# A two-block transformer kernel: the second layer's adaLN columns summed on VectorE instead of multiplied on TensorE

## The chip, the cores and the metric

The kernel is one program on one core of a Trainium2 chip. The metric is the device time of one execution in microseconds (us), lower is better; the runs shown are three executions of the kernel before. TensorE (PE) multiplies, VectorE (DVE), ScalarE (ACT) and GpSimd (POOL) do the elementwise work, and SyncE's queue (SP) issues the weight transfers.

## What is computed

The reference runs a first block of two layers on 256 latent tokens and 256 context tokens, and then a second block (gated mixing, a linear recurrence and a convolved feed-forward) on the latent tokens. All is fp32, with a model width of 2048. The part that the change touches is the modulation ahead of each layer of the first block:

```
shift, scale, gate = jnp.split(jax.nn.silu(c) @ ada_w[l] + ada_b[l], 3, axis=-1)
shift_c, scale_c, gate_c = jnp.split(jax.nn.silu(c_ctx) @ ada_w[l] + ada_b[l], 3, axis=-1)
h = rmsnorm(x, norm_g[l]) * (1.0 + scale[:, None]) + shift[:, None]
hc = rmsnorm(xc, norm_g[l]) * (1.0 + scale_c) + shift_c
...
x_new = x + gate[:, None] * out
```

Two vectors (`c` and `c_ctx`, 2048 long) are multiplied with a 2048 x 6144 matrix for each of two layers. In the last layer the context's gate is not used.

## The kernel before, in words

All weights stream from memory in chunks of 512 KB into the eight slots of `RAW`. A chunk of a projection ("tm" or "fm") is split by ACT (L1540, the high part) and DVE (L1784, the low part) into one of four `SPL` slots, and PE multiplies it in three products. A chunk of adaLN weights ("ada") isn't split: PE multiplies it from `RAW` with four column tiles side by side (L1289), 256 rows of the matrix and 512 columns at a time. Eight such chunks make a group of 512 columns; there are 12 groups for each layer: 0 to 3 shift, 4 to 7 scale, 8 to 11 gate. When a group is through, ACT copies its sums out of bank 6 (L1550), PE turns them (L1368, four transposes into bank 7), and DVE reduces them and adds the bias (L1814, L1818; L1822 for a scale).

The order of all work is written out by hand, by one planner. `chunks` holds the chunks in the order in which PE takes them; `run_chunks` walks it, and at each chunk it lets `run_ahead` put the loads and splits of coming chunks (up to five positions ahead, ada chunks counted), pops side tasks from `hi` and `low` (norms, rope, attention in rows of four stages, pooling, Fourier maps) and puts the matmuls. Each engine works off the one list `order` in that order, so whatever stands ahead on an engine's list comes first. A `RAW` slot is loaded again when the chunk eight places earlier has been split or multiplied (`load_ahead`); the loads stand in one queue, in chunk order.

The stretches of `chunks` are these. The first holds the first layer's eight shift and scale groups and the first k and v projection (72 chunks). Then come 64 projection chunks of the first layer (queries, pooling, Fourier, and from the 33rd on the gates), mixed by `mixed` with 64 ada chunks: two projection chunks, two ada chunks, and so on. Then 28 chunks of the output projection, mixed with 28 ada chunks, and four of it alone, which are multiplied in two passes (latent rows last). Then `FILL` = 4 ada chunks alone. Then the second layer's 72 projection chunks (two groups of queries, 16 chunks; k and v, 8; pooling, 8; Fourier, 8; gates, 32), mixed two and two with the last 32 ada chunks. A projection chunk of the first layer is 24 matmuls of 512 columns, one of the second layer's query, pooling and Fourier groups is 12.

At the second layer's start, each of the tiles of h is made by DVE (L1828), ACT (L1558, L1561) and POOL (L2237), and PE waits for them in order. `STAT`, `TMP` and the like are small buffers; `CW` holds silu(c) and silu(c_ctx) as columns.

Of the kernel before, what the change touches and what calls it, by code (L numbers as in the profile page):

```python
# [17 lines left out]
NRAW = 8  # L18
NSPL = 4
AHEAD = 5  # L20
START_AHEAD = 3
FILL = 4
# [37 lines left out]
def two_block_program(nc, I, out):  # L60
    es = ExitStack()
    with es:
# [114 lines left out]
        s_tab, s_dft = [sem(f"rope{l}_in") for l in range(2)], [sem(f"dft{l}_in") for l in range(2)]  # L177
        s_ap = [sem(f"pool_matrix{l}_in") for l in range(2)]
# [7 lines left out]
        s_adaE, s_adaT, s_adaS, s_ada, s_s2 = sem("ada_out"), sem("ada_turned"), sem("ada_summed"), sem("ada_column"), sem("ada_scale")  # L186
        s_h0, s_h1, s_h1b, s_h2 = sem("h_scaled"), sem("h_hi"), sem("h_shifted"), sem("h_lo")
# [44 lines left out]
        at = {"loaded": 0, "taken": 0, "split": 0, "used": 0, "pos": 0, "ahead": AHEAD}  # L232
# [13 lines left out]
        def multiplied():  # L246
            return (s_chunk, at["pos"])
# [7 lines left out]
        def group(form, stage, W, c0, banks, then, tokens=(), side=1):  # L255
            g = Group(form, stage, banks, tokens, side)
            aps = fm_aps(W, c0) if form == "fm" else tm_aps(W, c0)
            cs = [Chunk(g, kc, ap, {"ada": 0, "tm": 2, "fm": 4}[form]) for kc, ap in enumerate(aps)]
# [3 lines left out]

        def load_ahead():
            while at["loaded"] < len(queue):
                i = at["loaded"] - NRAW
                last = []
                if i >= 0 and queue[i].shape:
                    if i >= at["taken"]:
                        return
                    last = [(s_lo, split_no[i])]  # L270
                elif i >= 0:
                    if i >= at["pos"]:
                        return
                    last = [(s_chunk, i + 1)]
                put("load", i=at["loaded"], last=last)
                at["loaded"] += 1

        def run_ahead():
            load_ahead()
            while at["taken"] < min(len(queue), at["pos"] + (START_AHEAD if at["pos"] < 72 else at["ahead"])):  # L280
                i = at["taken"]
                if queue[i].shape:
# [4 lines left out]
                    last = [(s_chunk, chunk_split[at["split"] - NSPL] + 1)] if at["split"] > NSPL else []  # L287
# [18 lines left out]
        def flush(q):  # L306
            while q:
                q.pop(0)()
# [8 lines left out]
        def run_chunks(upto):  # L317
            while at["pos"] < upto:
                i = at["pos"]
                run_ahead()  # L320
                c = chunks[i]
                parts = 2 if c.shape and (c.group.wide or len(c.group.banks) == 4) and c.group.src is None else 1
# [16 lines left out]
                at["pos"] = i + 1  # L339
                at["used"] += c.shape > 0  # L340
                if c.then:
                    c.then()

# [11 lines left out]
        def mixed(main, left):  # L355
            seq = []
            for c in main:
                seq.append(c)
                if len(seq) % 4 == 2:
# [2023 lines left out]
```

## Time and profile before

| | us |
|---|---|
| three runs | 2348.18, 2350.48, 2351.04 |
| median of the runs | 2350.48 |
| span of the profiled execution, first to last instruction | 2348.8 |
| PE busy | 2272.0 (97%) |
| DVE busy | 1288.4 (55%) |
| ACT busy | 1042.1 (44%) |
| POOL busy | 269.0 (11%) |

The page gives the profiled execution by its span alone, which lies within the three runs' times. The page's first part is busy time by engine, its second part cuts the span in 40 slices of 58.7 us and gives the busy tenths of each engine; a granted clock of 9 or more is full speed. Its fourth part follows the chain that ended last. A line number is that of the kernel before.

### The profile page before, as it was taken

The page shows a single profiled execution, that of the slowest core. Times are in us where ns is not written, and L with a number is a line of the kernel's source. Part 1 is how long each engine was busy: PE and PEld are TensorE (multiplying, and loading weights), DVE is VectorE, ACT ScalarE, POOL GpSimd, SP SyncE. Part 2 cuts the span into 40 slices and gives each one's busy share as a digit, 9 for nine tenths or more (in the row PEclk, how much of TensorE's full clock was granted, in tenths as well). Part 3 has the DMA queues.
Part 4 walks back from the last instruction along what each step waited for, and adds up shares of the span by engine and source line. Part 5 has one row for each costly group of instructions (what it writes and reads, how often), then busy time and mean ns, then how long its engine had stood idle before and what let it go on. Part 6 is the DMA issues. An engine that isn't in the chain of part 4 may idle for free.

```text
span 2348.8 us, 30025 instructions
## 1 busy us (share of the span) xinstructions
PE 2272.0 (97%) x11859; PEld 1830.4 (78%) x11859; DVE 1288.4 (55%) x2030; ACT 1042.1 (44%) x1596; POOL 269.0 (11%) x326
## 2 busy tenths in 40 slices
PE   5899999999999999999999998999999999999998
PEld 2477777777777867678888887888888888888887
DVE  3354523332332264555776776667765777567764
ACT  2233333332322255445554565555544555345553
POOL 1010100000010122100020324111100111001111
PEclk9999999999999999999999998999999999999999
DMA  9974433445655475634566544565655555555553
GB/s 350 341 263 157 149 126 114 139 132 167 243 179 172 134 276 194 237 96 159 181 207 204 172 143 153 179 196 180 189 195 190 187 185 184 198 188 188 188 189 116
DMA packets 322427, 437.14 MB, mean 186 GB/s; under 512 B 13848, under 2 KB 220112, under 8 KB 321264
## 3 DMA queue, kind: packets, MB, share of 16 engines
q1 hardware_dynamic: 316800, 413.19, 53.2%
q0 software_dynamic: 3392, 16.90, 1.9%
q10 hardware_dynamic: 2096, 5.15, 0.6%
q8 instruction: 94, 1.54, 0.3%
q14 instruction: 45, 0.37, 0.0%
HBM read 428.89 MB, written 6.29 MB: 185 GB/s over the span
## 4 chain that ended last, share of the span: by engine, by line
PE 87%; DVE 4%; ACT 3%; DMA 3%; issue 1%; POOL 1%; SPq 0%; ACTq 0%; POOLq 0%
PE ps L1334 24%; PE ps L1335 12%; PE ps L1309 9%; PE ps L1311 8%; PE ps L1310 8%; PE ps L1329 5%; PE ps L1330 5%; PE ps L1331 5%; PE ps L1289 3%; PE ps L1383 1%; DVE SPL L1784 1%; ACT SPL L1540 1%; PE ps L1400 1%; DMA RAW<-in_ada_w_dram 1%; PE ps L1390 1%
## 5 line engine op out<-in xcount | busy, mean ns | idle before, releaser
L1784 DVE TENSOR_TENSOR SPL<-RAW,SPL 128x1024 fp32r<-128x1024 f32 x592 | 751.6, 1274 | 598.4 <-ACT SPL L1540 596.1
L1334 PE MATMUL ps<-HS,SPL 128*128 128x512 f32 x2688 | 957.7, 401 | 10.8 <-DVE SPL L1784 7.8
L1540 ACT ACTIVATE SPL<-RAW 128x1024 fp32r<-128x1024 f32 x592 | 622.1, 1055 | 493.2 <-PE ps L1311 170.9
L1335 PE MATMUL ps<-HS,SPL 128*128 128x256 f32 x2688 | 755.3, 281 | 0.0
L1334 PEld LDWEIGHTS ps<-HS,SPL 128*128 128x128 f32 x2688 | 507.7, 189 | 135.4 <-DVE SPL L1784 5.6
L1335 PEld LDWEIGHTS ps<-HS,SPL 128*128 128x128 f32 x2688 | 510.5, 190 | 2.0 <-issue 1.7
L1309 PE MATMUL ps<-SPL,HS 128*128 128x512 f32 x960 | 396.8, 413 | 12.2 <-DVE SPL L1784 5.3
L1311 PE MATMUL ps<-SPL,HS 128*128 128x512 f32 x960 | 377.1, 393 | 0.0
L1310 PE MATMUL ps<-SPL,HS 128*128 128x512 f32 x960 | 376.9, 393 | 0.0
L1309 PEld LDWEIGHTS ps<-SPL,HS 128*128 128x128 f32 x960 | 182.1, 190 | 75.5 <-issue 17.5
L1310 PEld LDWEIGHTS ps<-SPL,HS 128*128 128x128 f32 x960 | 182.3, 190 | 41.8 <-issue 6.3
L1311 PEld LDWEIGHTS ps<-SPL,HS 128*128 128x128 f32 x960 | 181.9, 189 | 39.5
L1329 PE MATMUL ps<-HS,SPL 128*128 128x512 f32 x480 | 194.7, 406 | 1.2 <-DVE HS L1940 1.2
L1331 PE MATMUL ps<-HS,SPL 128*128 128x512 f32 x480 | 187.1, 390 | 0.0
L1330 PE MATMUL ps<-HS,SPL 128*128 128x512 f32 x480 | 187.1, 390 | 0.0
L2287 POOL TENSOR_TENSOR MM<-MM,GX 128x256 f32<-128x256 f32 x96 | 60.4, 649 | 650.1 <-DVE MM L1921 650.1
L1289 PE MATMUL ps<-RAW,CW 128*32 128x512 f32 x768 | 110.8, 632 | 11.1 <-DMA RAW<-in_ada_w_dram 9.1
L1329 PEld LDWEIGHTS ps<-HS,SPL 128*128 128x128 f32 x480 | 90.1, 188 | 39.0 <-issue 13.2
L1331 PEld LDWEIGHTS ps<-HS,SPL 128*128 128x128 f32 x480 | 90.1, 188 | 19.4
L1330 PEld LDWEIGHTS ps<-HS,SPL 128*128 128x128 f32 x480 | 90.2, 188 | 18.2 <-issue 1.0
L2280 POOL TENSOR_TENSOR TMP<-TMP 128x256 f32<-128x256 f32 (+1 forms) x53 | 53.6, 1011 | 426.4 <-ACT TMP L1675 424.0
L1675 ACT ACTIVATE TMP<-XT 128x256 f32<-128x256 f32 (+1 forms) x58 | 26.7, 468 | 140.8 <-DVE XT L1952 109.4
(281 smaller groups left out, 1689.3 us busy)
## 6 DMA issues: line engine op xcount, KB each, us to landing
RAW<-in_w_in_dram SPq DMA_DIRECT2D x208, 512.0 KB, 5.7
RAW<-in_ada_w_dram SPq DMA_DIRECT2D x192, 512.0 KB, 4.9
RAW<-in_ffn_w_up_dram SPq DMA_DIRECT2D x192, 512.0 KB, 3.5
RAW<-in_w_out_dram SPq DMA_DIRECT2D x96, 512.0 KB, 4.5
RAW<-in_ffn_w_down_dram SPq DMA_DIRECT2D x96, 512.0 KB, 4.1
x_spill<-XT POOLq DMA_DIRECT2D x2, 2048.0 KB, 15.3
XT<-x_spill POOLq DMA_DIRECT2D x1, 4096.0 KB, 17.4
MM<-in_x_dram ACTq DMA_DIRECT2D x2, 1024.0 KB, 10.8
```

What stands on the lines that cost most here:

```text
L1289: m = mm(PS[6][32 * q:32 * q + 32, :], CW[:, 2 * k:2 * k + 32], raw_of(i)[:, kk * 512:(kk + 1) * 512], start=kc < 2, stop=kc >= 6, skip_gr ...
L1309: mm(PS[b][:, :], hr, wr, start=k == 0, stop=False, skip_group_check=True)
L1310: mm(PS[b][:, :], hr, wl, start=False, stop=False, skip_group_check=True)
L1311: m = mm(PS[b][:, :], hl, wr, start=False, stop=k == KT - 1, skip_group_check=True)
L1329: mm(PS[b][:, :], wr, hr, start=k == 0, stop=False, skip_group_check=True)
L1330: mm(PS[b][:, :], wr, hl, start=False, stop=False, skip_group_check=True)
L1331: m = mm(PS[b][:, :], wl, hr, start=False, stop=k == KT - 1, skip_group_check=True)
L1334: mm(PS[b][:, :], wr, hh, start=k == 0, stop=False, skip_group_check=True)
L1335: m = mm(PS[b][:, 256:512], wl, hh[:, 0:256], start=False, stop=k == KT - 1, skip_group_check=True)
L1540: act(SPL[:, (n - 1) % NSPL, 0, :], raw_of(i), ACT.Copy).then_inc(s_hi, 1)
L1784: tt(w[:, 1, :], raw_of(s["i"]), w[:, 0, :].bitcast(F32), ALU.subtract).then_inc(s_lo, 1)
L2287: tt(o, o, RSB, ALU.mult).then_inc(s_js, 1)
```

## The change

The first layer's gate groups stay as they are: 32 ada chunks, two behind every second projection chunk. The 96 chunks of the second layer are taken from PE. Each is now a "sum" chunk: DVE multiplies each of its two 128 x 512 tiles with one column of `CW` and adds it to an accumulator of 128 x 512, for each of the two vectors (one vector for the gate groups). The accumulators of a group are the two halves of `RAW` slot 6 or 7, in turn, so that the queue has six `RAW` slots from the first sum chunk to behind the last. When a group is through, PE transposes each accumulator (four transposes into bank 6), and DVE reduces 128 x 512 to 128 x 4 and adds the bias.

`mixed` now puts one sum chunk behind each projection chunk (and a second behind every twelfth in the first layer's stretch): 35 stand between the last 32 projection chunks of the first layer, 28 in its output projection, and 33 between the first 33 projection chunks of the second layer. Scale groups come first, then shift, then gate. `FILL` is 0: the second layer's first projection chunk follows the output projection at once. Loads into slots 6 and 7 behind the last sum wait until the last accumulators have been turned.

```diff
-FILL = 4
+NSUM = 6
+FILL = 0
...
+                free = range(NSUM if sums[0] <= i < sums[-1] + NRAW else NRAW)
...
+                    if raw_slot[i] >= NSUM and at["sums"]:
+                        if len(sums_turns) < at["sums"] or at["pos"] <= last_sum():
+                            return
+                        last = last + [(s_accT, len(sums_turns))]
...
+            put("ada_sum", i=i, kc=c.kc, half=g.half, before=done, last=last if c.kc == 0 else [])
...
-            for c in main:
+            for i, c in enumerate(main):
                 seq.append(c)
-                if len(seq) % 4 == 2:
-                    seq.extend(left[:2])
-                    del left[:2]
+                if left and left[0].shape == 0:
+                    n = 2 if i % 2 else 0
+                else:
+                    n = 2 if more and i % more == more - 1 else 1
+                seq.extend(left[:n])
+                del left[:n]
...
+            vectors = 1 if l and g >= 8 else 2
...
+                for v in range(vectors):
+                    hi.insert(3 + v, turn(v))
...
-        left = [c for g in range(8, 12) for c in ada_group(0, g)] + [c for g in range(12) for c in ada_group(1, g)]
+        left = [c for g in range(8, 12) for c in ada_group(0, g)] + [c for g in (*range(4, 8), *range(4), *range(8, 12)) for c in ada_sums(1, g)]
...
-        lay_out(main0[0] + mixed(main0[1], left))
+        lay_out(main0[0] + mixed(main0[1], left, 12))
...
+                elif kind == "sum_turn":
+                    e.wait_ge(*s["sums"])
+                    for b in range(4):
+                        o = slice(b * 128, (b + 1) * 128)
+                        m = turn(PS[6][:, o], sums_of(s["half"], s["v"])[:, o], IDN[:, :])
+                    m.then_inc(s_accT, 1)
...
+                    for kk in range(2):
+                        w = raw_of(i)[:, kk * 512:(kk + 1) * 512]
+                        for v, (sm, before) in enumerate(s["before"]):
+                            acc, c = sums_of(half, v), CW[:, 4 * kc + 2 * kk + v:4 * kc + 2 * kk + v + 1]
+                            if kc == 0 and kk == 0:
+                                ts(acc, w, c, None, ALU.mult).then_inc(sm, 1)
+                            else:
+                                e.wait_ge(sm, before + kk)
+                                stt(acc, w, c, acc, ALU.mult, ALU.add).then_inc(sm, 1)
...
+                    nc.vector.tensor_reduce(a[:, :, v], PS[6][:, :].rearrange("p (b q) -> p b q", b=4), AX_X, ALU.add).then_inc(s_adaS, 1)
```

Some pairs of semaphores (rope tables, Fourier tables, pooling matrices of the two layers) become one each, with the same waits counted on.

## Rows read from the trace of the kernel before

**Rows 1.** The page, part 2: busy tenths in 40 slices of the span
```profile
PE   5899999999999999999999998999999999999998
DVE  3354523332332264555776776667765777567764
```

**Rows 2.** Chain of waits, output projection: start us, us, engine, line (x8: one ada pair)
```profile
707.33 1.00 PE ps L1289 x8
708.33 0.43 PE ps L1329
719.43 1.00 PE ps L1289 x8
...
732.00 1.00 PE ps L1289 x8
```

**Rows 3.** Timeline of PE there, two matmuls in a row: start us, us
```profile
703.77 0.39 PE L1329 MATMUL ps<-HS,SPL 128*128 128x512 f32 x1
...
704.00 0.39 PE L1330 MATMUL ps<-HS,SPL 128*128 128x512 f32 x1
```

**Rows 4.** Stretches: us, busy us by engine (x count), granted clock, DMA share, GB/s
```profile
450.00:500.00 50.00, 50.00 (x262) 38.50 (x260) 21.37 (x52) 22.98 (x39) 0.00 (x0) 1.00 0.38 125
619.50:793.00 173.50, 171.49 (x804) 128.80 (x805) 59.62 (x81) 47.12 (x62) 15.75 (x12) 1.00 0.57 194
819.40:885.70 66.30, 60.52 (x302) 41.00 (x301) 41.58 (x72) 38.52 (x62) 16.87 (x21) 0.97 0.77 272
885.70:935.00 49.30, 49.30 (x236) 37.42 (x236) 23.24 (x38) 23.43 (x42) 13.76 (x16) 1.00 0.52 180
935.00:985.00 50.00, 45.45 (x222) 31.59 (x214) 29.08 (x56) 24.89 (x43) 9.31 (x10) 1.00 0.79 272
839.00:843.00 4.00, 2.51 (x15) 2.28 (x16) 2.10 (x3) 3.80 (x8) 1.32 (x2) 0.97 0.79 261
843.00:847.00 4.00, 4.00 (x13) 3.13 (x12) 2.75 (x5) 1.43 (x3) 2.09 (x3) 0.60 1.01 361
```

**Rows 5.** Chain of waits at the second layer's start
```profile
820.46 3.49 DMA RAW<-in_w_in_dram
...
828.62 0.51 PE ps L1309
```

**Rows 6.** Timeline of DVE where the gates end and the output projection starts
```profile
620.12 1.29 DVE L1916 TENSOR_TENSOR MM<-MM,TMP 128x512 f32<-128x512 f32 x2 [10.36 <-ACT TMP L1644]
...
622.25 9.72 DVE L1940 TENSOR_TENSOR HS<-MM,HS 128x512 fp32r<-128x512 f32 x16
```

**Rows 7.** Groups of DVE by form: busy us, mean ns of one, idle before
```profile
L2056 DVE SCALAR_TENSOR_TENSOR MM<-TMP,MM 128x512 f32<-128x512 f32 x4 | 2.8, 692 | 5.9 <-ACT TMP L1714 5.9
...
L1861 DVE TENSOR_REDUCE SM<-TMP 128x4 f32<-128x512 f32 x12 | 8.1, 679 | 0.7 <-ACT TMP L1588 0.7
```

**Rows 8.** Timeline of DVE: one behind the one it needs, then behind one it doesn't
```profile
862.94 0.69 DVE L1871 TENSOR_TENSOR MM<-MM,SM 128x512 f32<-128x512 f32 x1 [0.90 <-POOL SM L2248]
863.67 0.69 DVE L1880 TENSOR_TENSOR TMP<-MM 128x512 f32<-128x512 f32 x1
864.28 0.76 DVE L1882 TENSOR_TENSOR TMP<-MM 128x256 f32<-128x256 f32 x2
```

**Rows 9.** DVE's groups in 438 to 510 us, where attention rows run beside the gates
```profile
L1909 DVE COPY MM<-ps 128x128 f32<-128x128 f32 x13 | 3.8, 290 | 21.6 <-PE ps L1400 21.6
```

**Rows 10.** DVE's groups in 819.4 to 885.7 us, two of those that waited
```profile
L1784 DVE TENSOR_TENSOR SPL<-RAW,SPL 128x1024 fp32r<-128x1024 f32 x18 | 21.9, 1223 | 21.9 <-ACT SPL L1540 21.9
L1828 DVE SCALAR_TENSOR_TENSOR TMP<-XT,S,ps 128x256 f32<-128x256 f32 x18 | 8.0, 476 | 2.4 <-POOL HS L2237 2.4
```

**Rows 11.** Timelines of DVE and of POOL, where two-input operations of both overlap
```profile
907.21 1.85 DVE L1882 TENSOR_TENSOR TMP<-MM 128x256 f32<-128x256 f32 x2
...
906.74 2.04 POOL L2237 TENSOR_TENSOR HS<-TMP,HS 128x256 fp32r<-128x256 f32 x2 [2.95 <-ACT TMP L1561]
```

More of the change, by code:

```diff
@@ L231, in two_block_program @@
         slots = [(i, []) for i in range(4)]
-        at = {"loaded": 0, "taken": 0, "split": 0, "used": 0, "pos": 0, "ahead": AHEAD}
+        at = {"loaded": 0, "taken": 0, "split": 0, "used": 0, "pos": 0, "ahead": AHEAD, "multiplied": 0, "summed": [0, 0], "sums": 0}
+        raw_slot, raw_nth, raw_before = [], [], []
+        after_chunk = {}
+        sums_last, sums_turns = {}, {}
         split_no, chunk_split = {}, {}
@@ L286, in run_ahead @@
                     split_no[i], chunk_split[at["split"]] = at["split"], i
-                    last = [(s_chunk, chunk_split[at["split"] - NSPL] + 1)] if at["split"] > NSPL else []
+                    last = after_chunk[chunk_split[at["split"] - NSPL]] if at["split"] > NSPL else []
                     put("split", i=i, last=last)
@@ L338, in run_chunks, with chunk_multiplied, sums_first, sum_chunk @@
                     put("mm", i=i, c=c, inputs=inputs, after=after, banks=range(part * half, (part + 1) * half), end=part == parts - 1, src=c.group.src)
-                at["pos"] = i + 1
-                at["used"] += c.shape > 0
+                chunk_multiplied(i)
                 if c.then:
                     c.then()
+        def chunk_multiplied(i):
+            at["pos"] = i + 1
+            at["multiplied"] += 1
+            after_chunk[i] = [multiplied()]
+            at["used"] += chunks[i].shape > 0
+        def sums_first(half):
+            b = max(j for j in range(at["pos"]) if raw_slot[j] == NSUM + half)
+            return [(s_lo, split_no[b])] if queue[b].shape > 1 else after_chunk[b]
+        def sum_chunk(i, c):
+            g = c.group
+            if c.kc == 0:
+                if g.half not in sums_last:
+                    sums_last[g.half] = sums_first(g.half)
+                last = sums_last[g.half]
+                while last and last[0] is None:
+                    hi.pop(0)()
+                    last = sums_last[g.half]
+            done = []
+            for v in range(g.vectors):
+                done.append((s_acc[v], at["summed"][v]))
+                at["summed"][v] += 2
+            put("ada_sum", i=i, kc=c.kc, half=g.half, before=done, last=last if c.kc == 0 else [])
+            after_chunk[i] = [(s_acc[g.vectors - 1], at["summed"][g.vectors - 1])]
+            at["pos"] = i + 1
+            if c.then:
+                c.then()
         def staged(tasks):
@@ L368, in two_block_program, with ada_sums, after, turn @@
         ada_ready, s2_ready = {}, {}
+        def ada_sums(l, g):
+            vectors = 1 if l and g >= 8 else 2
+            half = ada_sums.count % 2
+            ada_sums.count += 1
+            def after():
+                sums = [(s_acc[v], at["summed"][v]) for v in range(vectors)]
+                at["sums"] += vectors
+                sums_last[half] = [None]
+                def turn(v):
+                    z = {}
+                    def f():
+                        s = put("sum_turn", l=l, g=g, v=v, half=half, sums=sums[v], after=use(6), end=v == vectors - 1, vectors=vectors)
+                        sums_turns[l, g, v] = s["n"]
+                        bank_last[6] = [(s_adaS, tick("ada_sum_out"))]
+                        if v == vectors - 1:
+                            sums_last[half] = [(s_accT, s["n"])]
+                            s["out"] = tick("ada_out_columns")
+                            ada_ready[l, g] = (s_ada, s["out"])
+                            if 4 <= g < 8:
+                                s2_ready[l, g - 4] = (s_s2, tick("s2"))
+                        s["sum_no"] = count["ada_sum_out"]
+                    return f
+                while len(hi) < 3:
+                    hi.append(idle)
+                for v in range(vectors):
+                    hi.insert(3 + v, turn(v))
+            cs = group("sum", "ada", I["ada_w"][l, :, :], g * 512, [], after, side=0)
+            cs[0].group.half, cs[0].group.vectors = half, vectors
+            return cs
+        ada_sums.count = 0
         def ada_group(l, g, side=0):
```

116 lines of the change are left out of this document (72 added, 44 removed).

## Prediction

> **What bounds the kernel now.** I read the busy tenths first: PE stands at nine tenths in nearly all slices, DVE mostly at two or three in slices 6 to 13, the first layer, and at four to seven behind it [rows 1]. So in the first layer DVE is spare, and time that leaves PE there leaves the span, if nothing else comes late. Next the chain of waits in the output projection, to price an ada pair where PE never stops: the pair takes 1.00 us, and the matmul behind it 0.43 us [rows 2] where one starts 0.23 us behind another otherwise [rows 3]. A pair costs 1.00 + 0.20 = 1.2 us. Then the stretches: in 619.5 to 793 PE is busy 171.49 of 173.5 us and DVE 59.62; at the second layer's entrance, 819.4 to 885.7, PE 60.52 and DVE 41.58 of 66.3 us [rows 4]. There the chain shows PE waiting behind the fill for a transfer, 3.49 us, and for the tiles of h until 828.62 [rows 5].
>
> **PE in the first layer.** Of the 48 pairs that leave PE, 30 stood before 819.4 us: 16 in the gates' stretch, 14 in the output projection. The last of the gates' stretch lay in a wait for the output projection's tiles, which started at 622.25 [rows 6], and brings nothing. 29 x 1.2 = 34.8 us go. Against this a group of two vectors is turned twice instead of once. A turn costs 0.47 us: two pairs stand 12.57 us apart with a turn between them (719.43 to 732.00) and 12.10 without (707.33 to 719.43) [rows 2]. Seven groups end here in both kernels: 7 x 0.47 = 3.3 us more.
>
> **What DVE gets.** No row shows the new accumulation (a tile times a column, plus another tile, 512 wide). The nearest is a scalar_tensor_tensor of that width, 692 ns [rows 7]; from start to start it is 0.73 us behind one that it needs and 0.61 us behind one that it doesn't [rows 8]. With two vectors in turn I take 0.61, so 4 x 0.61 = 2.5 us for a chunk; with one vector, each waits for the last, 2 x 0.73 = 1.46 us. In all 64 x 2.5 + 32 x 1.46 = 207 us. Each of the 20 accumulators adds a reduction, 0.68 us [rows 7].
>
> **Is it hidden in the first layer?** In 619.5 to 793, 28 x 2.5 = 70 us join the 59.6 [rows 4], and the stretch shrinks by 14 pairs to 157 us: 130 of 157, with splits put two projection chunks, some 11 us, ahead. Hidden. Beside the gates, 13 rows of attention run in 72 us [rows 9], and DVE is busy 21.37 of 50 us [rows 4]. There the scaling of a row's exponentials may come to stand behind a sum and a split, 2.5 + 1.2 = 3.7 us, and the half chunk that covers it is 12 x 0.23 = 2.7 us with a row's own work on top. I take 1 us in all for late rows; the bounds are none and 13 rows by the 1.2 us that a split adds, 16 us. At the gates' end one sum stands on DVE's list between the last gating (over at 620.12 + 1.29 = 621.4) and the output projection's tiles: these start at 623.9 instead of 622.25 [rows 6], 1.7 us later. First layer: -34.8 + 3.3 + 1.0 + 1.7 = -28.8 us.
>
> **The second layer's entrance,** 16 query chunks. PE loses 8 pairs (9.6 us), the fill (2.4), and, the first projection chunk being four places earlier in the queue, the 3.49 us for its transfer [rows 5]: alone it would need some 51 us. DVE gets one double sum (2.5), 16 single ones (23.4) and five reductions (five at 0.5 net, 2.5): 41.6 + 28.4 = 70.0 us. Its 21.9 us of waits for splits [rows 10] are where this fits; its other waits, 2.4 us for POOL's tiles [rows 10] and 1.6 of small ones, I leave: 74 us, so DVE ends last. It also meets POOL, busy for 16.87 us here [rows 4]. Two DVE operations of 256 columns took 1.85 us beside POOL, and POOL's two 2.04 us [rows 11], where DVE's took 0.76 us alone [rows 8]. The accumulations read two SBUF tiles, as those do. Between nothing and the whole 16.9 us I take 3, near the lower end, because POOL's tiles follow DVE's in a chain. 77 for 66.3: +10.7 us.
>
> The Trainium skill ("SBUF — State Buffer", the section on the shared port pair) says that a DVE operation with two SBUF inputs and a GpSimd operation shut each other out for a whole instruction, which speaks against this change. The overlapping rows agree where the two met. By the rule taken fully, all of POOL's time would be serial with DVE's, and the entrance 91 us instead of 77.
>
> **Behind the entrance.** In the k and v stretch four pairs go, 4.8 us; DVE has 23.2 + 8 x 1.46 + 0.5 = 35.4 of 44.5 us, POOL 13.8 [rows 4]. I take 3 of the 4.8. In pooling, 935 to 985, four more go; DVE has 29.1 + 8 x 1.46 = 40.8 of 45 us [rows 4], with attention rows that pass from engine to engine: I take 2 of 4.8. For both the bounds are all and none. Then, loads into slots 6 and 7 wait until the last accumulator is turned, some four chunks behind the last sum. They hold up all loads behind them, and ACT stands at the split of the first: one landing, like the 3.49 us above [rows 5] at most; I take 2, between 0 and 5. That the queue has six slots costs nothing more, by my reading: a load stands one and a half projection chunks, 8 us, ahead of its split in the first layer, and in the entrance DVE ends last. Second layer: +10.7 - 3 - 2 + 2 = +7.7 us.
>
> **The sum.** -28.8 + 7.7 = -21.1 us on the span of 2348.8: 2327.7. The median of the runs is 1.7 us above that span, so 2329.4; I say 2330.
>
> **The rivals.**
> A. The second layer keeps its gain too: the sums fill DVE's 21.9 us of waits [rows 10] and PE ends last. Against it: 28.4 us are added. The entrance would gain some 10 us and the rest 9: 2350.5 - 28.8 - 19 = 2303.
> B. DVE delays the attention rows by the upper bound, 16 us: 2330 + 16 = 2346, no change that can be told. For it: DVE's 2.5 us come between each two rows. Against: the splits and rows are put well ahead.
> C. The other side. DVE starves PE at the entrance: 74 us with all of POOL's 16.9, 91 us, of which PE, at 51, works little more than half. After a stretch of 4 us in which it was busy 2.51, its granted clock was 0.60 in the next four [rows 4], where it does the work of 2.4 us in 4; five such are 8 us. The entrance is 33 us longer, k and v and pooling gain nothing, 2 for the slots: 2350.5 - 28.8 + 35 = 2357. It turns the sign once the second layer loses 29 us.
> D. The pairs cost PE nothing, because transfers or splits set the pace: no change, 2350. Against it: nothing but PE stands in the chain between two pairs [rows 2], and DMA is at 0.57 in that stretch [rows 4].
>
> **How the numbers follow.** The forecast has 62%, between 2318 and 2343; A 14%, B 10%, C 10%, D 4%. 2306 to 2350 leaves out half of A, nearly all of C and the edges of the rest. A measurement of this kernel tells 0.2%, about 4.7 us, from no change. Faster by more: 0.62 + 0.14 + half of B, 0.81. Within: the rest of B and D, 0.10. Slower: C, 0.09.
>
> **What would show it.** In the trace after: the first layer's output projection with two chunks in 10.9 us and no idle time of PE; accumulations 0.61 us apart with two vectors, 0.73 with one; the first layer's end at 819.4 - 28.8 = 790.6; then query chunks whose matmuls wait for DVE's low parts, DVE busy for nine tenths, for some 77 us. I am wrong if an accumulation costs well over 0.75 us, if PE waits in the attention rows, or if PE and not DVE ends last at the entrance.

## Result and profile after

| us | before | after |
|---|---|---|
| median | 2350.54 | 2428.38 |
| lowest to highest | 2348.18 to 2351.04 | 2424.33 to 2430.32 |
| span of the profiled execution | 2348.8 | 2422.5 |
| PE busy | 2272.0 (97%) | 2255.6 (93%) |
| DVE busy | 1288.4 (55%) | 1517.9 (63%) |

The ratio is 1.0332, with a 95% interval of 1.0318 to 1.0347: the changed kernel is 3.3% slower, where 0.9% faster was forecast. PE did lose work, 16 us of busy time, and the span grew by 74.

The busy tenths of the kernel after, and its granted clock in tenths (slices of 60.6 us), answer to [rows 1]:

```profile
PE   5899999889799867789999998999999999999998
...
DVE  3354524666777667654676867667764677557764
...
PEclk9999999999899988999999999999999999999999
```

From slice 8 to 18 PE has eight digits of six to eight, where it had nines. DVE is at five to seven there, far from full. Neither engine is full in this stretch, so something passes between them that takes its time. From PE's timeline I took where the stretches begin and end; the lengths are differences of its rows:

| stretch, us | before | after |
|---|---|---|
| first layer's gates, from 395 | 224.1 | 245.6 |
| join to the output projection | 3.6 | 5.4 |
| output projection, 28 chunks | 170.8 | 177.7 |
| its last four (end of the first layer) | 25.5 (at 819.4) | 26.9 (at 851.3) |
| second layer's 16 query chunks | 65.3 | 89.1 |
| k and v | 50.1 | 54.6 |
| pooling and Fourier, to the first gate matmul | 84.6 (at 1019.5) | 99.5 (at 1094.5) |
| the rest, to the end of the span | 1329.3 | 1328.0 |

All of the loss lies before 1094.5 us. PE's waits there, summed by what released them (line waited for: us in total, times, longest), first for 395 to 860 us and then for 851 to 1095:

```profile
PE ps L1470 <- DVE ADA L1949: 24.0, 6, 5.9
PE ps L1529 <- ACT TMP L1741: 7.4, 1, 7.4
PE ps L1424 <- DVE HS L2069: 5.4, 1, 5.4
PE ps L1404 <- DVE XT L2081: 3.7, 1, 3.7
...
PE ps L1477 <- DVE MM L2014: 13.9, 3, 8.8
PE ps L1477 <- DVE MM L2017: 7.5, 1, 7.5
PE ps L1404 <- DVE SPL L1898: 6.2, 4, 3.3
PE ps L1404 <- POOL HS L2366: 6.0, 1, 6.0
PE ps L1470 <- DVE RAW L1943: 5.1, 1, 5.1
```

Line 1470 is the turn of an accumulator; 1477 is the norm ahead of attention, 1485 and 1502 are attention, 1529 is the Fourier map, and 1404 and 1424 are projections. What is behind them shows in the chain of waits of the output projection, 690 to 730 us (start us, us, engine, what); it answers to [rows 2], in which only PE stood:

```profile
701.55 4.75 DVE RAW L1943 x4
706.31 0.37 SPq L1351
706.67 0.04 issue
706.72 5.22 DMA RAW<-in_w_out_dram
711.94 0.02 issue
711.96 1.07 ACT SPL L1642
713.03 0.02 issue
713.06 0.04 DVE SPL L1898
713.09 1.11 issue
714.20 2.74 DVE RAW L1943 x4
716.96 0.37 SPq L1351
717.33 0.04 issue
717.37 5.15 DMA RAW<-in_w_out_dram
```

This is a closed loop. The sums of a chunk (L1943) free its slot; SP issues the next adaLN load into it and behind that a projection load (in_w_out); the projection chunk lands 5.2 us later; ACT splits it, 1.07; DVE makes its low part, some 1.1; and only then does DVE come to the next sums, because its list says so. One turn of it, from one issue to the next in the chain, is 706.31 to 716.96, 10.65 us. Two projection chunks pass in a turn, and their matmuls take 10.9 us (two in 10.9 us is also what the forecast had for the stretch). So the loop has 0.3 us of slack, and nearly all that is added to it is paid. What is added stands in the timeline of DVE, SP and POOL a little earlier (start us, us, engine, line, what, [idle before]):

```profile
691.35 0.68 DVE L1949 TENSOR_REDUCE ADA<-ps 128x4 f32<-128x512 f32 x1
691.95 2.73 DVE L1943 SCALAR_TENSOR_TENSOR RAW<-RAW,CW 128x512 f32<-128x512 f32 x4
692.09 0.65 PE L1470 MATMUL ps<-IDN,RAW 128*128 128x128 f32 x4 [4.04 <-DVE ADA L1949]
694.71 0.37 SPq L1351 DMA_DIRECT2D RAW<-in_ada_w_dram  x1
...
699.89 1.66 DVE L2081 SCALAR_TENSOR_TENSOR XT<-ps,ADA,XT 128x256 f32<-128x256 f32 x4 [3.12 <-PE ps L1426]
701.46 4.82 DVE L1943 SCALAR_TENSOR_TENSOR RAW<-RAW,CW 128x512 f32<-128x512 f32 x4
701.51 3.55 POOL L2409 TENSOR_TENSOR TMP<-TMP 128x512 f32<-128x512 f32 x2 [24.39 <-ACT TMP L1777]
706.31 0.37 SPq L1351 DMA_DIRECT2D RAW<-in_ada_w_dram  x1
```

The output's addition to x is 1.66 us, a reduction 0.68, and four accumulations beside two POOL operations take 4.82 instead of 2.73. The Trainium skill ("SBUF — State Buffer", "Who interferes with whom") has a DVE instruction with two SBUF inputs and a GpSimd instruction that reads SBUF shut each other out. POOL's two would take 2.56 us alone (1.28 each, measured in e10), and DVE's take 2.09 more: the trace agrees in the main.

At 692.09 PE waits 4.04 us for the second turn of a group: bank 6 is free once DVE has reduced the first accumulator, and this reduction stands on DVE's list behind a low part whose chunk had yet to land. Behind such a wait PE is slow for a while. Two windows of 4 us after it (us, busy us by engine (x count), granted clock, DMA share, GB/s):

```profile
693.00:697.00 4.00, 4.00 (x12) 3.10 (x12) 3.67 (x6) 1.06 (x1) 0.00 (x0) 0.57 0.30 67
697.00:701.00 4.00, 4.00 (x19) 3.30 (x18) 1.11 (x3) 0.20 (x1) 0.00 (x0) 1.00 0.58 199
```

Twelve matmuls instead of nineteen: a wait of 4 us costs another 1.6 us by the clock (an estimate: seven matmuls by 0.23 us). The stretches that answer to [rows 4], in the same columns: the output projection, the entrance, and k and v.

```profile
646.80:824.50 177.70, 164.29 (x697) 134.38 (x698) 134.36 (x180) 40.66 (x48) 18.50 (x11) 0.94 0.56 181
851.30:940.40 89.10, 59.88 (x226) 46.96 (x226) 63.56 (x100) 36.50 (x60) 21.53 (x22) 0.83 0.50 168
940.40:995.00 54.60, 47.13 (x205) 37.69 (x203) 36.02 (x54) 22.98 (x37) 14.13 (x16) 0.94 0.55 181
```

At the entrance DVE is busy for 63.6 of 89.1 us, so it isn't the bound that the forecast saw. The chain there, 851 to 940 us, by its largest shares:

```profile
by line: DMA RAW<-in_w_in_dram 40.3%; DVE RAW L1943 14.1%; issue 12.4%; ACT SPL L1642 9.5%; SPq L1351 2.9%; DVE TMP L1957 2.8%; ACT HS L1660 2.1%; ACT TMP L1663 1.8%; POOL HS L2366 1.8%; DVE SPL L1898 1.7%; DVE MM L2000 1.6%; DVE TMP L2009 
```

It is the same loop: landings, and sums that hold up the loads. A query chunk here is 12 matmuls, so PE needs only 24 x 0.23 = 5.5 us for the two chunks that pass in a turn (an estimate from [rows 3]), against a turn of some 9 us or more: 4.7 for the landing, 1.1 and 1.15 for the two parts, 0.4 for the issue and 1.5 or more for the sums.

### The profile page after: what moved, and what is told of

Its sections match the earlier page's. It is cut to its first block, busy times and chain, and to the rows that moved or that the text cites. A ratio compares the mean times of both kernels' runs of the same rounds, so it can differ in the third digit from the quotient of the medians.

```text
span 2422.5 us, 29721 instructions
## 1 busy us (share of the span) xinstructions
PE 2255.6 (93%) x11507; PEld 1851.6 (76%) x11507; DVE 1517.9 (63%) x2358; ACT 1038.8 (43%) x1584; POOL 276.2 (11%) x326
## 4 chain that ended last, share of the span: by engine, by line
PE 71%; DVE 10%; DMA 9%; ACT 4%; issue 3%; POOL 1%; SPq 1%; ACTq 0%; POOLq 0%; DVEq 0%
PE ps L1429 23%; PE ps L1430 12%; PE ps L1404 8%; PE ps L1406 8%; PE ps L1405 8%; DMA RAW<-in_w_in_dram 5%; DVE RAW L1943 4%; DMA RAW<-in_w_out_dram 3%; ACT SPL L1642 3%; DVE SPL L1898 2%; PE ps L1424 2%; PE ps L1384 2%; PE ps L1425 2%; PE ps L1426 2%; PE ps L1485 1%
## 5 line engine op out<-in xcount | busy, mean ns | idle before, releaser
L1404 PE MATMUL ps<-SPL,HS 128*128 128x512 f32 x960 | 402.1, 419 | 27.1 <-DVE SPL L1898 11.5
L1406 PE MATMUL ps<-SPL,HS 128*128 128x512 f32 x960 | 381.6, 397 | 0.0
L1405 PE MATMUL ps<-SPL,HS 128*128 128x512 f32 x960 | 381.5, 397 | 0.0
L1404 PEld LDWEIGHTS ps<-SPL,HS 128*128 128x128 f32 x960 | 185.5, 193 | 85.3 <-DVE SPL L1898 17.9
L1943 DVE SCALAR_TENSOR_TENSOR RAW<-RAW,CW 128x512 f32<-128x512 f32 x300 | 223.1, 793 | 1.1
L1405 PEld LDWEIGHTS ps<-SPL,HS 128*128 128x128 f32 x960 | 185.5, 193 | 42.6 <-issue 6.3
L1406 PEld LDWEIGHTS ps<-SPL,HS 128*128 128x128 f32 x960 | 184.7, 192 | 40.8
L1424 PE MATMUL ps<-HS,SPL 128*128 128x512 f32 x480 | 200.2, 417 | 9.0 <-DVE HS L2069 5.4
L1424 PEld LDWEIGHTS ps<-HS,SPL 128*128 128x128 f32 x480 | 94.3, 197 | 30.4 <-issue 6.7
L2271 DVE SCALAR_TENSOR_TENSOR MM<-MM,VV 128x256 f32<-128x256 f32 x192 | 79.8, 473 | 1.2 <-ACT MM L1842 1.2
## 6 DMA issues: line engine op xcount, KB each, us to landing
MM<-in_x_dram ACTq DMA_DIRECT2D x2, 1024.0 KB, 10.9
```

Source lines behind the costliest of these rows:

```text
L1404: mm(PS[b][:, :], hr, wr, start=k == 0, stop=False, skip_group_check=True)
L1405: mm(PS[b][:, :], hr, wl, start=False, stop=False, skip_group_check=True)
L1406: m = mm(PS[b][:, :], hl, wr, start=False, stop=k == KT - 1, skip_group_check=True)
L1424: mm(PS[b][:, :], wr, hr, start=k == 0, stop=False, skip_group_check=True)
L1943: stt(acc, w, c, acc, ALU.mult, ALU.add).then_inc(sm, 1)
L2271: stt(o, CV[c][:, tap:tap + 256], V(c_fw[tap] + col), o, ALU.mult, ALU.add).then_inc(s_ct, 1)
```

## The experiments

All ratios are to the kernel before, run on the same chip; a span is that of the profiled execution. A profiled execution can lie some us off its kernel's median: e9's was 7.0 us below it, the kernel after's 4.1 below, e3's 4.3 above, the others within 3. Line numbers shift by a few between kernels. The edits are to the changed kernel.

### How far ahead the splits stand, and the sums' own time

```diff
+        def near():
+            among = any(c.shape == 1 for c in queue[at["pos"]:at["pos"] + 2])
+            return 3 if among and at["ahead"] == AHEAD else at["ahead"]
...
-            while at["taken"] < min(len(queue), at["pos"] + (START_AHEAD if at["pos"] < 72 else at["ahead"])):
+            while at["taken"] < min(len(queue), at["pos"] + (START_AHEAD if at["pos"] < 72 else near())):
```

> Edit: while sums stand among the coming chunks, splits are put two positions ahead instead of four; nothing else. Theory L (a loop through the load queue): a projection chunk's load stands behind the load of the sum chunk ahead of it, which waits for a sum six places back; the split of that projection chunk stands on DVE's list in front of the next sums. With splits four positions ahead, two projection chunks pass in one turn of the loop: issue 0.4, landing 5.2, high part 1.07, low part 1.2, sum 2.73, some 11 us (all from the trace of the changed kernel), against 10.9 us of matmuls, so every gating, addition or POOL stall in the loop is paid in full. With two positions ahead three chunks pass in the same 11 us, and the first layer gets back nearly all of the 60 us by which it missed the forecast, the second layer's entrance some 10 us: 2350 to 2370. Theory D (DVE has too much work, or POOL's port stalls it): the same work in the same order of sums, no change, 2425 to 2435. Theory T (TensorE waits at the second turn of a group for DVE's reduction): no change, or worse, since splits come later.

Measured: 2376.37 us, ratio 1.0110 (1.0095 to 1.0125), span 2373.2. A split that stands later on the lists lets the sums ahead of it run first and free their slots sooner. That is how I read it. The one number of the planner gives back 52 of the 78 us, a little less than expected: the entrance goes from 89.1 to 71.4, pooling from 99.5 to 86.5. The output projection stays at 178.7, now with PE's waits at splits (14.6 us in seven waits): there the split comes too late.

```diff
-                            acc, c = sums_of(half, v), CW[:, 4 * kc + 2 * kk + v:4 * kc + 2 * kk + v + 1]
+                            acc, w = sums_of(half, v)[:, 0:16], raw_of(i)[:, kk * 512:kk * 512 + 16]
+                            c = CW[:, 4 * kc + 2 * kk + v:4 * kc + 2 * kk + v + 1]
```

> Edit: each accumulation works on 16 columns instead of 512, so most of the sums are left out; all loads, slots, waits and turns stay. Theory L: a loop turn loses 2.4 of 11 us and fits under the 10.9 us of matmuls; theory D too takes away its cause: both say 2325 to 2345 (forecast of the entrance included). Theory S (six slots and the order of loads are too few by themselves, whatever DVE does): above 2400.

Measured: 2373.65 us, ratio 1.0096 (1.0080 to 1.0111), span 2371.3. This kernel leaves out 496 of each 512 columns of the sums, and is still 23 us slower than before; no range above holds that. The output projection falls to 157.5 us, as the loop has it: without most of the sums' 2.7 us a turn fits well under PE's 10.9. The first layer ends at 811.3. But the entrance takes 81.8 and pooling 95.4: in the second layer a turn is longer than PE's two chunks even without the sums' work, which the expectation had not asked. The chain of the entrance, 811.3 to 892.9 us:

```profile
by line: DMA RAW<-in_w_in_dram 34.7%; issue 14.3%; ACT SPL L1642 11.7%; DVE SPL L1898 5.4%; DVE RAW L1944 4.9%; DVE TMP L1958 4.1%; ACT HS L1660 3.5%; SPq L1351 1.8%; DVE MM L2001 1.7%; DVE TMP L2010 1.7%; DVE TMP L2012 1.7%; PE ps L1404 1.
```

Landings still lead it. Six slots, loads in one order and the turns cost this much without DVE's work on the sums.

### The two turns apart, and the second layer's gates on PE

```diff
+                gap = 1 if g == 3 else 3
+                while len(hi) < 2 + gap:
+                    hi.append(idle)
                 for v in range(vectors):
-                    hi.insert(3 + v, turn(v))
+                    hi.insert(3 + gap * v, turn(v))
```

> Edit: the two turns of a group's accumulators are put three side tasks apart instead of one (but for the last shift group, whose result is needed at once). Theory T: the waits of 4 to 5 us of TensorE at the second turn of each group, seven times before 851 us, vanish: 2395 to 2405. Theory L: they are only the place where TensorE meets DVE's delay; within 8 us of the changed kernel, 2420 to 2435.

Measured: 2410.41 us, ratio 1.0255 (1.0237 to 1.0272), span 2412.8; by the medians 18 us of the 78, between the two theories' ranges. In the first layer the turns no longer wait for each other (24.0 us of such waits without the edit), but PE waits 16.2 us for splits instead, in 13 places: the loop stays. In the second layer two waits of 5.0 and 4.4 us at turns are left.

```diff
-        left = [c for g in range(8, 12) for c in ada_group(0, g)] + [c for g in (*range(4, 8), *range(4), *range(8, 12)) for c in ada_sums(1, g)]
+        left = [c for g in range(8, 12) for c in ada_group(0, g)] + [c for g in (*range(4, 8), *range(4)) for c in ada_sums(1, g)] + [c for g in range(8, 12) for c in ada_group(1, g)]
...
-        lay_out(mixed(main1[1], left))
+        lay_out([main1[1][0], left.pop(0)] + main1[1][1:6] + mixed(main1[1][6:], left))
```

> Edit: the second layer's four gate groups go back to TensorE, in pairs behind every second projection chunk from the sixth on; shift and scale stay sums. The changed kernel lost some 43 us behind the end of the first layer (22.7 at the entrance, 5.4 in k and v, 15 in pooling). If single-vector sums cause that, all but a few us come back: 2380 to 2392. If the missing fill and the sums of the first layer's end cause it (tiles of h late), at most 10 us come back: above 2415.

Measured: 2391.90 us, ratio 1.0182 (1.0166 to 1.0197), span 2388.9. The second layer is back near before (69.7, 49.9 and 87.4 us against 65.3, 50.1 and 84.6), while the first layer keeps its whole loss and ends at 853.5. Of the 78 us, 41 are left, and 34 of them are there at the first layer's end, where the forecast had a gain of 29. So the second layer's loss goes when its loads no longer wait for sums; whether it was the waiting or the work, e5 tells.

### The order of the loads

In e5 the load of a sum chunk stands in the queue behind the load of the projection chunk three places on, instead of ahead of it. The slots are the same six, and so are the lists of ACT, DVE and PE.

```diff
+            while load_next(False) or load_next(True):
+                pass
...
+            if i == len(queue) or (of_sums and at[False] <= i + 3):
+                return False
```

> Edit: in the load queue, each sum chunk's load is put behind the load of the projection chunk three places further on, so that no projection chunk's load waits for a recent sum; splits stand four positions ahead as in the changed kernel, all work is the same. Theory L: the loop of 11 us is gone without touching DVE's order, so at least what the nearer splits gave (52 us) comes back, and the waits for late splits that these brought (2.2 us each) don't appear: 2350 to 2372. Theory D (DVE's work or POOL's port sets the pace, and the nearer splits only changed the order in DVE's favour): above 2400. The waits at the second turn stay in either.

Measured: 2365.18 us, ratio 1.0058 (1.0043 to 1.0073), span 2364.3: 63 of the 78 us come back from the order of one queue. The output projection takes 157.5 us instead of 177.7, the entrance 73.4 instead of 89.1, and no landing is among the chain's twelve largest shares at the entrance any more. SP still waits for sums (104 us of the output projection, 160 in the kernel after), but the next projection loads stand ahead of the ones that wait.

> Edit: the load order of the run before and, with it, the two turns of a group three side tasks apart. In the changed kernel the turns apart were worth 18 us. If TensorE's wait at the second turn is a cost of its own, 10 to 18 us below the run before: 2335 to 2355. If it was part of the load loop, within 4 us of that run.

Measured, with e3's edit on top of e5: 2351.75 us, ratio 1.0010 (1.0001 to 1.0020), span 2349.8, level with before. The 28 output chunks, 631.10 to 788.50, and below them the entrance:

```profile
631.10:788.50 157.40, 157.40 (x705) 130.27 (x705) 135.06 (x183) 38.63 (x45) 18.52 (x11) 0.99 0.59 191
...
812.60:885.90 73.30, 57.67 (x226) 46.27 (x226) 64.65 (x101) 36.71 (x61) 22.66 (x23) 0.84 0.69 224
```

PE never stops in the first, with DVE busy for 135.06 us: the same sums that cost 20 us with the loads in one order cost nothing here (e5, with the turns as they were, has 157.5 too).

> Edit: later load order, turns apart, and accumulations on 16 columns (most of the sums left out), against the same kernel with full sums (2351.8). If what is left of the loss is DVE's work (and its meetings with POOL), 2320 to 2332: the forecast's sum without the entrance's excess. If it is slots and the missing fill, within 8 us of 2352.

e9 is e6 with e2's narrow accumulations, so it too leaves out most of the sums. Measured: 2326.72 us, ratio 0.9903 (0.9886 to 0.9919), span 2317.9. And e1 with the same narrowing:

> Edit: splits two positions ahead and accumulations on 16 columns (most of the sums are left out). No load loop and hardly any work of sums. Against the run with nearer splits alone (2376), the difference is what DVE's work itself and its meetings with POOL cost: by the forecast's sum 15 to 20 us in the entrance alone. Expected 2325 to 2345. If it stays near 2370, something else of the change (six slots, turns, the missing fill) holds the time.

Measured: 2341.06 us, ratio 0.9960 (0.9946 to 0.9975), span 2337.8. The sums' own work costs 32 us of span in e6 and 35 in e1; by the medians 25 and 35.

e5, e6 and e9 differ by one edit each, so that the four spans part the loss:

| us | e9 | e6 | e5 | after | before |
|---|---|---|---|---|---|
| end of the first layer | 798.0 | 812.6 | 825.1 | 851.3 | 819.4 |
| from there to the first gate matmul | 192.8 | 207.8 | 208.4 | 243.2 | 200.1 |
| span | 2317.9 | 2349.8 | 2364.3 | 2422.5 | 2348.8 |

From e9 to e6, the sums' own work: 31.9 us. To e5, turns that are close: 14.5. To the kernel after, loads in one order: 58.2, 26.2 in the first layer and 34.8 in the second, less 2.7 behind it. By the medians the three parts are 25.0, 13.4 and 63.2. They also hang on the order in which they are taken: with the loads in one order and the turns close, narrow sums give back 51 us of span (e2), and what is then left to e9 is 53.

### Fewer sums, in other places

The kernels from here on build on e6 and keep the second layer's gates on PE; in the first layer, e7 and e11 have 64 sums, e10 32, e12 24, e13 56. The number given to mixed says behind every how many projection chunks a second sum chunk follows.

```diff
-        lay_out(mixed(outs0[:28], left) + outs0[28:])
+        lay_out(mixed(outs0[:28], left, 28) + outs0[28:])
```

> Edit: load order and turns as in the run before; one more sum chunk at the end of the first layer, so that all 64 shift and scale sums are there; the four gate groups go back to TensorE in the second layer. The first layer keeps its gain (some 29 us by the forecast's sum, less what is left of late rows), the second layer is as before but for the missing fill: 2322 to 2342, under the kernel before. If sums in the first layer can't gain (DVE and POOL meeting there), 2350 or more.

Measured: 2366.06 us, ratio 1.0067 (1.0052 to 1.0082), span 2365.7. It is slower than e6, and the doubled sum at the very end of the mixed stretch does it: PE stands 13.7 us at one turn behind it, and the last four chunks take 43.9 us instead of 25.2.

> Edit: sums only where DVE is idlest and TensorE never stops. The second layer's scale groups are multiplied on TensorE beside the gates, as before; its four shift groups (32 chunks) are summed on DVE in the first 26 chunks of the output projection; its gate groups are multiplied on TensorE in the second layer, as before; later load order and turns apart stay; no fill. By rows: 14 pairs go from the output projection (16.8 us), four groups are turned once more (1.9), the second layer without fill is some 3 us longer (202.8 for 200), the step from eight slots to six costs up to 5: 2338 to 2346, faster than the kernel before. If sums can't be hidden even there, 2350 or more.

Measured, with `mixed(outs0[:26], sums, 4)`: 2394.95 us, ratio 1.0189 (1.0174 to 1.0204). The miss of the series: half the sums, and a worse time. The gates' stretch is as before, 224.1 us, and the output projection takes 213.4. PE's waits in it, 620 to 840 us, show where:

```profile
PE ps L1439 <- DVE SPL L1913: 29.0, 17, 3.0
PE ps L1485 <- DVE RAW L1958: 6.9, 2, 5.7
```

One sum behind each projection chunk lets the two kinds alternate in six slots, so that a projection chunk finds a slot that a split frees. A doubled place shifts this by one: followed through `place_raw`, the three projection chunks behind it get a slot that a sum frees. With a doubled place behind every fourth chunk that is three chunks of four: 29.0 us in 17 waits, and the clock with them (0.92 in the stretch).

> Edit: sums of all 64 shift and scale chunks in the first layer, the last one two projection chunks before the end of the mixed stretch, gate groups on TensorE in the second layer. In the run with the last sum at the very end, TensorE waited 13.7 us at its turn. That goes: 2347 to 2352. Against the run with sums in the output projection alone, it shows what sums beside the gates are worth: if they gain, it is the faster of the two; if the attention rows eat the gain, slower by 5 to 10 us.

Measured, with three doubled places (8 instead of 4) and the other sums beside the gates: 2372.53 us, ratio 1.0097 (1.0082 to 1.0113). The output projection takes 183.4. Nine projection chunks stand behind its doubled places, and PE waits six times for splits in it, at most 2.7 us:

```profile
PE ps L1438 <- DVE SPL L1912: 11.7, 6, 2.7
```

The last four chunks are back at 25.7 us, as expected, but the whole is 20 us above its range. It is faster than e10 by the output projection alone: the gates' stretch takes 234.4 us against 224.1, with 16 pairs fewer in it.

```diff
-                    n = 2 if i % 2 else 0
+                    n = 4 if i in more else 2 if i % 2 else 0
...
-                    n = 2 if more and i % more == more - 1 else 1
+                    n = 1
...
-        left = [c for g in range(8, 12) for c in ada_group(0, g)] + [c for g in range(4, 8) for c in ada_group(1, g)]
+        left = [c for g in range(8, 12) for c in ada_group(0, g)] + [c for g in (4, 5, 6, 7, 0) for c in ada_group(1, g)]
+        left += [c for g in (1, 2, 3) for c in ada_sums(1, g)]
...
-        lay_out(main0[0] + mixed(main0[1], left, 12))
+        lay_out(main0[0] + mixed(main0[1], left, (9, 23, 37, 51)))
...
-        lay_out(mixed(outs0[:26], sums, 4) + outs0[26:])
+        lay_out(mixed(outs0[:26], left) + outs0[26:])
```

> Edit: as the run with sums in the output projection alone, but only 24 chunks (three groups), exactly one behind each of its first 24 projection chunks; the 72 other chunks that come before them are multiplied on TensorE beside the gates (four double pairs), the gate groups in the second layer. Theory P (parity of slots): with six slots and one sum behind each projection chunk, projection chunks and sums each keep their own three slots; a second sum in a place shifts them, a projection chunk's load then waits for a sum, and the loop is back. That is why six extra sums made the output projection 213 us. Evenly spaced it is 158 to 162, the whole 2340 to 2348. Theory Q (five or more sums in four chunks are just too much for DVE and POOL, or the load order rule fails there for another reason): the output projection stays above 170.

The edit is to e10. Here mixed puts exactly one sum behind each of the first 24 output chunks, and four pairs of adaLN chunks more on PE beside the queries to gates, at the places given. Measured: 2355.95 us, ratio 1.0016 (1.0005 to 1.0028), span 2353.3. Six doubled places, 213.4 us; three, 183.4; none, 156.7, with 24 sums. The number of sums isn't what does it: e6 has 28 in this stretch and none doubled, and takes 157.4; e11 has 29 and 183.4. e12's stretch:

```profile
642.50:799.20 156.70, 155.56 (x697) 128.50 (x698) 128.36 (x173) 43.37 (x54) 17.69 (x11) 1.00 0.62 209
```

The gain of the output projection, 14.1 us, is there in full. But the gates end at 638.0 us instead of 619.4, and four pairs are 4.8 of that.

> Edit: 56 chunks (seven groups) as sums, exactly one behind each of the last 30 chunks beside the gates and the first 26 of the output projection; 40 chunks on TensorE ahead of them, the gate groups on TensorE in the second layer. Theory P: output projection 158 to 162; gates 222 to 228 (229 with three doubled places and without three more pairs); the second layer 203: 2338 to 2347. Theory Q: output projection above 170.

Measured: 56 sums, strictly one to one, from the gates on: 2356.50 us, ratio 1.0013 (1.0004 to 1.0023). The gates' stretch is 235.0 us, 11 more than before, though 15 pairs have left it (18 us). It isn't the same work, though: PE has 1118 matmuls in it, e6 1008, so side tasks have moved into it from the stretch ahead, where three places have two pairs of adaLN chunks. To the gates' end e13 is 7.8 us later than before, with twelve pairs fewer (14 us). So sums beside the gates bring no gain, strict or not; how much of this is the sums' and how much comes from those three places, no run parts. The output projection takes 164.4, with 3.7 us at one turn.

### Where e12's gain went

e14 and e15 move e12's four doubled places: to (51, 55, 59, 63), and to (57, 59, 61, 63).

> The 24 sums beside the output projection as in e12_even_outs, 72 adaLN chunks on PE beside the first layer's queries to gates; the four places with two pairs of them lie behind its 52nd, 56th, 60th and 64th projection chunk instead of its 10th, 24th, 38th and 52nd. Theory Q (the 14 us that e12 lost ahead of the output projection were the doubled pairs' own: they moved side tasks late, PE waited 4.6 us at 219 and its clock fell there and at 440): nearly all of this comes back, some 10 us, and what is left is the output projection's gain of 14 us less 4.8 for the four pairs and the 3 us that the second layer's entrance loses: ratio 0.996 to 0.998, some 2343. Theory R (six slots or the sums themselves cost time ahead of the output projection): as e12, 1.001 to 1.002. Theory S (doubled pairs cost the same wherever they stand, by the load queue): as e12 too, but with new PE waits of over 1 us in 570 to 640 us.

Measured: 2353.67 us, ratio 1.0012 (1.0003 to 1.0022), span 2352.6; the gates end at 631.6.

> As e14_pairs_late, with the four doubled places behind the 58th, 60th, 62nd and 64th projection chunk, where every second projection chunk is followed by four adaLN chunks on PE. Theory Q: as e14 within 2 us, since no attention rows are left there. Theory S: the load of a split chunk then stands behind four adaLN loads in a row, each needing a slot, and PE waits some 1 to 2 us at each place: 4 to 8 us slower than e14.

Measured: 2349.09 us, ratio 0.9992 (0.9983 to 1.0000), span 2344.6; the gates end at 621.9. So the places did it, not the sums or their slots. A stretch of 25 us in e12, and the same in the kernel before:

```profile
215.00:240.00 25.00, 20.99 (x87) 15.67 (x88) 12.59 (x20) 8.10 (x12) 2.92 (x2) 0.86 0.44 160
...
215.00:240.00 25.00, 25.00 (x123) 18.25 (x122) 9.75 (x20) 8.97 (x16) 0.74 (x1) 1.00 0.32 112
```

In it PE waits 4.6 us for DVE in one norm task, and its clock is lowered behind the wait. Attention and norm tasks are put beside projection chunks and not beside these adaLN chunks, so four of adaLN in a row shift the one against the other; that this makes the wait is my reading. At the very end, where no such task is left, doubled pairs cost their 4.8 us and no more: e15's gates take 228.9 us, 224.1 + 4.8. That density would cost by itself, as e15's second expectation had it, is out: it is 5 us faster than e14, where both theories had it level or slower. Why e14 came to only 2 of the 10 us expected is open; its gates took 234.9, with 3.2 us of waits for splits.

e15 is the best kernel here that does all the work, and at 0.08% it is not told from the kernel before. No version clearly beats it.

## Why the prediction was wrong, point by point

**What bounds the kernel; an ada pair costs PE 1.2 us.** Right. Where nothing waits, the output projection takes 157.4 us in e6 and 156.7 in e12; the forecast's own terms give 170.8 - 14 x 1.2 + 3 x 0.47 = 155.4. With the sums narrow and the loads apart (e9) the first layer ends 21.4 us earlier than before, of the 28.8 forecast; 5.5 of the 7.4 that are missing are one wait of PE beside the gates (below).

**A sum chunk costs 2.5 us.** Too low, but not what failed. The page of the kernel after, part 5 (xcount | busy, mean ns of one | idle before), answers to [rows 7]:

```profile
L1943 DVE SCALAR_TENSOR_TENSOR RAW<-RAW,CW 128x512 f32<-128x512 f32 x300 | 223.1, 793 | 1.1
```

Four take 2.73 us alone, 0.68 each and not the 0.61 that I took from [rows 8], and up to 4.8 beside POOL.

**"That the queue has six slots costs nothing more."** This is the step that failed, 58 of the 95 us between forecast and span. I had read that a load stands 8 us ahead of its split, and took this for enough, as a landing takes some 5. But a load of a projection chunk also stood behind a sum chunk's load in the one queue, and that waited for the sums, and these for the split before them. I had asked whether each queue had time on average (130 of 157 us on DVE), not what it takes to go round once: 0.4 for the issue, 5.25 for the landing, 1.1 and 1.15 for the two parts and 2.75 for the sums, 10.65 us, as much as PE's two chunks. All of it but the sums' time could be read in the trace of before, in which a chunk of this matrix lands in 4.5 us (median). The same step missed one thing more: with six slots, the three projection chunks behind each doubled place of `mixed` use a slot that a sum frees. In the change this touches mainly the gates' stretch.

**The first layer is hidden.** In the output projection it is, once the loads are apart (e6). Beside the gates it isn't: 229.4 us in e6 against 216.4 with narrow sums, 13 us (e9's profiled execution lies 7 us below its median, so this may be somewhat too much). The size is near the upper bound of rival B, 16, but late attention rows are the smaller part. PE's waits in this stretch are 15.7 us in e6 and 6.1 in e9. In e6, 12.1 of them stand where three projection chunks follow a doubled place (behind the 36th and the 60th chunk of the mixed stretch, and 0.3 behind the 48th), 2.4 in attention:

```profile
435.18 3.78 PE L1541 MATMUL ps<-XT 128*128 128x256 f32 x8 [7.69 <-ACT TMP L1753]
...
600.93 0.50 PE L1436 MATMUL ps<-HS,SPL 128*128 128x512 f32 x1 [1.05 <-DVE SPL L1910]
...
609.65 0.50 PE L1436 MATMUL ps<-HS,SPL 128*128 128x512 f32 x1 [2.98 <-DVE SPL L1910]
```

The first of these is the largest wait of the stretch, 5.5 us in e9 and 7.7 in e6. ACT stands at the split of the 39th chunk, whose slot the doubled sum had, and the Fourier map waits behind ACT. In e13, with no doubled sum, the only wait of a Fourier map there is 1.4 us. In the kernel after:

```profile
434.90 1.06 ACT L1642 ACTIVATE SPL<-RAW 128x1024 fp32r<-128x1024 f32 x1 [7.30 <-DMA RAW<-in_w_in_dram]
...
436.56 3.78 PE L1529 MATMUL ps<-XT 128*128 128x256 f32 x8 [7.40 <-ACT TMP L1741]
```

**A turn costs 0.47 us.** Its PE time does; its place wasn't asked. Two turns one task apart wait for each other through bank 6: 14.5 us of span from e5 to e6 (13.4 by the medians), 18 by the medians from the kernel after to e3. The forecast counted what a turn issues, and left out that the second waits for DVE's reduction of the first, with the low part queued ahead of it.

**The join, 1.7 us later.** 5.4 instead of 3.6, as forecast, though PE has a longer wait inside it (5.4 us at L1424).

**The entrance, 77 us, DVE the bound.** 89.1, and DVE idle for 25 of them. The chain goes through landings, not through DVE. Where the loads and turns are apart (e6) it takes 73.3, k and v 46.2 and pooling 88.3, which with the rest comes to 207.8 - 200.1 = +7.7 us for the second layer, the forecast's very number. That is partly luck: the entrance, k and v, and pooling are off by -3, -1 and +6 us, and the 2 us for slots 6 and 7 don't show. PE's clock of 0.84 at e6's entrance was not in the sum. The wait for x, 3.7 us (L1404 behind L2081), is in the entrance of every kernel measured; the forecast took the fill's 2.4 us away as if nothing had lain behind it.

**The rivals.** C had the sign and a mechanism near the true one at the entrance, and only 35 us for it; its main part, loads held up by sums, stood in none. D, that transfers set the pace, was dismissed on a chain in which only PE stood [rows 2] and a DMA share of 0.57 [rows 4]. The share is 0.56 after, with transfers on the chain: it tells of the engines' throughput, and not of how long one load has to wait for its slot.

**What stays open.** The 13 us beside the gates were parted by PE's waits alone, and no run has sums strictly one to one there without doubled pairs of adaLN chunks ahead of them. Nor was it tried to load the sum chunks through another queue, or to place their accumulators outside RAW.

## What to carry to other kernels

When a second consumer takes slots of a ring that one queue fills in order, write down the loop: consume, free, issue, land, convert, and back to the consumer's place on its list. Compare one turn with the time that the bound engine takes for what passes in it; shares of busy time say nothing about this. Loads of the work that isn't urgent belong behind the urgent ones, and kinds that alternate in a ring must do so strictly: with six slots, each doubled place here gave the next three urgent chunks a slot that the slow consumer frees.

## What was unexpected of the hardware

- A short wait of PE costs more than itself: 4.04 us idle, then 12 matmuls in 4 us at a granted clock of 0.57, where 19 run at 1.00.
- Four accumulations of 128 x 512 with their two inputs in SBUF took 2.73 us alone and 4.82 beside POOL's additions, and POOL's operation 1.78 each there against 1.28 alone in e10.
